# Scores of the second and third branch: one full f32 product a tile against three rounded products of high and low parts

## What is computed

```python
# second branch: 8 heads of 128, keys picked by an index (top 128 of 512, causal)
score = where(kpos <= t, sum_h iw_h * relu(iq_h . ik), -inf);  idx = top_k(score)
s = (q . k[idx]) * 128 ** -0.5 + bias;  p = masked_softmax(s);  o_b = p @ v[idx]

# third branch: 8 heads in 2 groups, three sources of keys: compressed (31 blocks),
# selected blocks (here all), window (here all causal keys)
o_c = softmax(q . k_cmp * scale, cmask) @ v_cmp
o_s = softmax(q . ks * scale + bias) @ vs
o_w = softmax(q . kw * scale + wbias) @ vw
o = gate0 * o_c + gate1 * o_s + gate2 * o_w
```

## Time and profile before

| | |
|---|---|
| median of 3 runs | 1434.14 us |
| the profiled execution | 1434.28 us, its span 1432.5 us |
| PE | busy 1421.0 us, 99% of the span, 7066 matmuls |
| DVE, ACT | busy 771.7 and 617.5 us, 54% and 43% |
| granted PE clock, mean | 0.999 |

### The profile page before, as it was taken

The page is one execution under the profiler, slowest core; times in us unless marked ns, Lnnn a source line. Parts: engine busy times, 40 slices in busy tenths (PEclk is TensorE's granted clock), DMA queues, the critical chain, the costliest instruction groups (busy, mean ns, idle before and its releaser), DMA issues.

```text
span 1432.5 us, 17397 instructions
## 1 busy us (share of the span) xinstructions
PE 1421.0 (99%) x7066; PEld 1156.6 (81%) x7066; DVE 771.7 (54%) x1326; ACT 617.5 (43%) x1013; POOL 82.8 (6%) x69
## 2 busy tenths in 40 slices
PE   9999999999999999999999999999999999999998
PEld 8867778887888888886777788887779888888886
DVE  6577857855243364465355244573355645656545
ACT  4455541225234343355346324453343654535342
POOL 0000000022120001000000110000000101001000
PEclk9999999999999999999999999999999999999999
DMA  6210223222322244541110424253123995768511
GB/s 202 64 46 32 74 89 117 89 88 75 102 65 82 70 145 150 176 132 45 31 59 30 162 88 147 90 176 103 59 89 127 244 239 139 197 172 184 168 74 59
DMA packets 127938, 160.42 MB, mean 112 GB/s; under 512 B 7365, under 2 KB 98754, under 8 KB 127603
## 3 DMA queue, kind: packets, MB, share of 16 engines
q1 hardware_dynamic: 117088, 133.51, 29.0%
q0 software_dynamic: 10624, 25.73, 8.3%
q10 hardware_dynamic: 146, 0.07, 0.0%
HBM read 155.06 MB, written 4.24 MB: 111 GB/s over the span
## 4 chain that ended last, share of the span: by engine, by line
PE 98%; DVE 1%; ACT 1%; issue 0%; DMA 0%; DVEq 0%; ACTq 0%
PE dense L809 24%; PE dense L811 24%; PE dense L810 24%; PE score L955 4%; PE score L972 3%; PE turned L972 3%; PE turned L955 2%; PE turned L965 1%; PE score L965 1%; PE score L809 1%; PE score L811 1%; PE score L810 1%; PE turned L811 1%; PE turned L809 1%; PE turned L810 1%; PE score L1126 1%
## 5 line engine op out<-in xcount | busy, mean ns | idle before, releaser
L809 PE MATMUL dense<-hidden_high,weight_high 128*128 128x512 f32 (+1 forms) x840 | 327.1, 389 | 0.0
L811 PE MATMUL dense<-hidden_high,weight_low 128*128 128x512 f32 (+1 forms) x840 | 320.7, 382 | 0.0
L810 PE MATMUL dense<-hidden_low,weight_high 128*128 128x512 f32 (+1 forms) x840 | 320.4, 381 | 0.0
L1495 ACT ACTIVATE weight_high<-raw 128x1024 fp32r<-128x1024 f32 (+5 forms) x178 | 211.9, 1227 | 218.5 <-PE dense L811 194.0
L2014 DVE TENSOR_TENSOR weight_low<-raw,weight_high 128x2048 fp32r<-128x2048 f32 (+2 forms) x78 | 158.9, 2046 | 192.5 <-ACT weight_high L1495 192.4
L811 PEld LDWEIGHTS dense<-hidden_high,weight_low 128*128 128x128 f32 x840 | 157.9, 188 | 30.8
L810 PEld LDWEIGHTS dense<-hidden_low,weight_high 128*128 128x128 f32 x840 | 158.2, 188 | 29.2 <-issue 0.5
L809 PEld LDWEIGHTS dense<-hidden_high,weight_high 128*128 128x128 f32 x840 | 158.1, 188 | 29.0 <-issue 0.5
L2009 DVE TENSOR_TENSOR weight_low<-raw,weight_high 128x1024 fp32r<-128x1024 f32 (+1 forms) x98 | 104.3, 1113 | 91.6 <-ACT weight_high L1495 91.6
L809 PE MATMUL dense<-weight_high,hidden_high 128*128 128x256 f32 (+1 forms) x288 | 82.0, 285 | 0.1
L811 PE MATMUL dense<-weight_high,hidden_low 128*128 128x256 f32 (+1 forms) x288 | 81.2, 282 | 0.0
(11 more groups left out here) (379 smaller groups left out, 2501.0 us busy)
## 6 DMA issues: line engine op xcount, KB each, us to landing
raw<-in_w_in SPq DMA_DIRECT2D x33, 1024.0 KB, 5.3
raw<-in_mlp_w SPq DMA_DIRECT2D x23, 1024.0 KB, 5.6
raw<-in_w_branch SPq DMA_DIRECT2D x12, 1024.0 KB, 5.3
down_raw<-in_mlp_w SPq DMA_DIRECT2D x12, 1024.0 KB, 6.1
raw<-in_mlp_w POOLq DMA_DIRECT2D x9, 1024.0 KB, 8.6
raw<-in_nsa_cmp_w SPq DMA_DIRECT2D x8, 1024.0 KB, 5.4
raw<-in_cross_wkv SPq DMA_DIRECT2D x8, 1024.0 KB, 5.2
down_raw<-in_mlp_w POOLq DMA_DIRECT2D x6, 1024.0 KB, 12.1
```

What stands on the lines that cost most here:

```text
L809: pe.matmul(out_ap, ah, bh, start=first, stop=False)
L810: pe.matmul(out_ap, ah, bl, start=False, stop=False)
L811: return pe.matmul(out_ap, al, bh, start=False, stop=last)
L1495: return nc.scalar.activation(dst, src, ACT.Copy, scale=scale)
```

## The change

Score tiles with 256, 384 and 512 keys, in the second and the third branch, are computed as three rounded products: high part of queries x high part of keys, high x low, low x high. Tiles with 128 keys, and the scores of the compressed keys, stay full f32 products, so the plain f32 values are kept as well: the first 128 tokens of queries and keys in the second branch, the first 128 of the keys and all of the queries (`qT`) in the third.

- ACT writes, per query product, a plain copy (256 elements a row in the second branch, 1024 as before in the third) and the rounded high part (1024).
- DVE waits for that (`query_high`), subtracts for the query's low part, and only this counts as the taking of the bank: the taker of `dq` and `nq` goes from "A" to "V".
- DVE writes three things per key product where it wrote one: the plain first 128 tokens, the high part, and, after waiting for it, the low part.
- In DVE's order, the query's low part stands ahead of the low part of slab + 2 and of the key's parts.
- The semaphore `up_relu_done`, which nothing used, gives its place to `query_high_ready`.

```diff
+        kTH = at("keys_high", [P, 2, T], 132, F32R)
+        dsaQ = [at("dsa_query_high", [P, 2, T], 128, F32R), at("dsa_query_low", [P, 2, T], 188, F32R), at("dsa_query_first", [P, 2, P], 196)]
+        dsaK = [kTH, at("dsa_key_low", [P, 2, T], 192, F32R), at("dsa_key_first", [P, 2, P], 197)]
+        nsaQ = [at("nsa_query_high", [P, 2, T], 178, F32R), at("nsa_query_low", [P, 2, T], 182, F32R), qT]
+        nsaK = [kTH, at("nsa_key_low", [P, 2, T], 200, F32R), at("nsa_key_first", [P, 2, P], 204)]
...
-            product(("dq", p), "A", slab_at["dq", p])
+            product(("dq", p), "V", slab_at["dq", p])
...
+            def split_terms(q, k, h, w, i):
+                rows, cols = slice(i * P, (i + 1) * P), slice(0, (i + 1) * P)
+                if i == 0:
+                    return [(q[2][:, h, rows], k[2][:, w, cols])]
+                return [(q[0][:, h, rows], k[0][:, w, cols]), (q[0][:, h, rows], k[1][:, w, cols]),
+                        (q[1][:, h, rows], k[0][:, w, cols])]
...
-                pe.wait_ge(taken["A"], taken_count[product_at["dq", p]])
+                pe.wait_ge(taken["V"], taken_count[product_at["dq", p]])
...
-                        score_tile((8 + 2 * p + h) * NT + j, [(qT[:, h, i * P:(i + 1) * P], kT[:, h, 0:(i + 1) * P])], (i + 1) * P)
+                        score_tile((8 + 2 * p + h) * NT + j, split_terms(dsaQ, dsaK, h, h, i), (i + 1) * P)
...
-                            score_tile(n, [(qT[:, h, i * P:(i + 1) * P], kT[:, w, 0:(i + 1) * P])], (i + 1) * P)
+                            score_tile(n, split_terms(nsaQ, nsaK, h, w, i), (i + 1) * P)
...
 # ScalarE, second branch
-                copy(qT[:, :, :], bank(("dq", p))[:, :, :], HEAD_SCALE).then_inc(taken["A"], 1)
+                copy(dsaQ[2][:, :, :], bank(("dq", p))[:, :, 0:P], HEAD_SCALE)
+                copy(dsaQ[0][:, :, :], bank(("dq", p))[:, :, :], HEAD_SCALE).then_inc(query_high, 1)
                 high(slab_at["dq", p] + 2)
...
 # ScalarE, third branch
             def nsa_query(p):
                 ready(("nq", p))
-                copy(qT[:, :, :], bank(("nq", p))[:, :, :], HEAD_SCALE).then_inc(taken["A"], 1)
+                copy(qT[:, :, :], bank(("nq", p))[:, :, :], HEAD_SCALE)
+                copy(nsaQ[0][:, :, :], bank(("nq", p))[:, :, :], HEAD_SCALE).then_inc(query_high, 1)
...
 # VectorE
+            def query_low(name, p, parts):
+                dve.wait_ge(query_high, p + 1 + (4 if name == "nq" else 0))
+                rest(parts[1][:, :, :], bank((name, p))[:, :, :], parts[0][:, :, :], HEAD_SCALE).then_inc(taken["V"], 1)
+
+            def key_parts(name, p, parts):
+                src = bank((name, p))
+                V.tensor_copy(parts[2][:, :, :], src[:, :, 0:P])
+                link(V.tensor_copy(parts[0][:, :, :], src[:, :, :]))
+                V.tensor_tensor(parts[1][:, :, :], src[:, :, :], parts[0][:, :, :].bitcast(F32), ALU.subtract).then_inc(taken["V"], 1)
+
             merge(0)
             for p in range(4):
+                query_low("dq", p, dsaQ)
                 low(slab_at["dq", p] + 2)
                 ready(("dk", p))
-                V.tensor_copy(kT[:, :, :], bank(("dk", p))[:, :, :]).then_inc(taken["V"], 1)
+                key_parts("dk", p, dsaK)
...
             def nsa_key(r):
                 ready(("kk", r))
                 dve.wait_ge(merge_added, GROUPS)
-                V.tensor_copy(kT[:, :, :], bank(("kk", r))[:, :, :]).then_inc(taken["V"], 1)
+                key_parts("kk", r, nsaK)
 
             for name, i in NSA_BEGIN:
+                if name == "nq":
+                    query_low("nq", i, nsaQ)
                 if name == "kk":
                     nsa_key(i)
                 if name != "vv":
                     low(slab_at[(name, *i) if name == "cw" else (name, i)] + 2)
...
             for p in range(4):
                 r = p // 2
+                if p:
+                    query_low("nq", p, nsaQ)
                 if p == 2:
                     low(slab_at["nq", p] + 2)
                     nsa_key(r)
```

More of the change, by code:

```diff
@@ L477, in layer @@
                 product("hidT", "A")
-            product((name, i), {"nq": "A", "kk": "V", "vv": "A"}[name], slab_at[name, i])
+            product((name, i), {"nq": "V", "kk": "V", "vv": "A"}[name], slab_at[name, i])
         product("cmp", "V")
         for name, i in (("nq", 1), ("nq", 2), ("kk", 1), ("vv", 1), ("nq", 3)):
-            product((name, i), {"nq": "A", "kk": "V", "vv": "A"}[name], slab_at[name, i])
+            product((name, i), {"nq": "V", "kk": "V", "vv": "A"}[name], slab_at[name, i])
         merge_products(2)
@@ L663, in layer @@
         up_ready = sem("up_ready")
-        up_relu_done = sem("up_relu_done")
+        query_high = sem("query_high_ready")
         up_summed = sem("up_sums_ready")
@@ L1207, in _ @@
                         nsa_v(r)
-                pe.wait_ge(taken["A"], taken_count[product_at["nq", p]])
+                pe.wait_ge(taken["V"], taken_count[product_at["nq", p]])
                 pe.wait_ge(taken["V"], taken_count[product_at["kk", r]])
```

## The result

The changed kernel takes 1436.57 us, the median of 20 runs (1435.59 to 1437.64); beside it the kernel before took 1434.43 (20 runs, 1433.99 to 1434.99). The ratio is 1.0015, interval 1.0008 to 1.0021: 0.15% slower. That is clear of the noise of 20 runs, and still inside the 0.2% that the prediction counts as no change. The profiled execution took 1436.6 us, its span 1434.8, 2.3 more than before.

A forecast was written before the change was run, and what follows sets the result against it. TensorE, busy 99% of the span, was taken as the bound. From 1434.28, less 6.2 in score bursts, plus 6.2 of waits and 1.9 for the clock, less 0.14 above the median: 1436.0 us; 8-in-10 range 1431.3 to 1439.0.

The forecast's parts named there:

- Matmul time: Score tiles, second and third branch: three rounded products for one full save 0.37 us in each of 24 sets, 8.8 us.
- What evictions take back: Score bursts: tiles wait for VectorE's eviction three tiles back, leaving 6.2 us saved, bounds 5.4 to 8.8.
- The walk: Tile-by-tile reckoning of score bursts, each tile no earlier than 0.32 us after the eviction three tiles back; gave 6.2 us saved.
- Hidden parts: Extra split work: zero in second branch and third-branch pair 2; pairs 1 and 3 together 0.1 us, each zero to 1.0.
- The gap ahead of key product 0: Third branch's opening: TensorE waits 4.5 us, the query's low part preceding the weights' on VectorE; bounds 3.5 to 5.5.
- The gap ahead of value product 0: Third branch's opening: three key instructions ahead of the weights' low part add 1.6 us of wait, bounds 1.2 to 2.0.
- The clock: TensorE's clock falls in the opening stall, key product 0 begins at half speed: 1.9 us, between zero and 4.8.
- Sum: Whole kernel: 1434.28 - 6.2 + 6.2 + 1.9 = 1436.2, less 0.14 above the median: 1436.0 us, 0.13% more.
- Matmul time alone: Rival, score bursts: no waits for evictions, clock kept, 8.8 us saved against 6.2 of stalls: 1431.5 us; chance 0.07.
- No stall at the opening: Rival, third branch: VectorE reaches the weights in time, only 1.6 + 0.1 us lost: 1429.6 us; chance 0.08.
- The clock low for all of 9.7 us: Rival, key product 0: 1.2 GHz throughout, 4.8 us lost, 1438.9 us; chance 0.26, shared with an unseen extra stall.
- Rounding without gain: Rival, score tiles: rounded products cost as much as full ones, bursts no shorter, about 1442 us; chance 0.01.

The follow-up runs named there:

- e3: Changed kernel with its split work kept, but each tile of 256 to 512 keys one full f32 product of the high parts: 1442.30 us, ratio 1.0056.
- e4: Changed kernel with two rounded products per tile of 256 to 512 keys, query low x key high left out: 1432.97 us, ratio 0.9990.
- e8: Kernel of e7 with tiles ordered 128, 384, 256, 512 keys, then 128, 512, 256, 384: 1425.73 us, ratio 0.9938.
- e7: Kernel of e5 with the low part of a head's output moved behind the last eviction of the scores: 1428.07 us, ratio 0.9955.
- e6: The change in the second branch alone, third branch as in the kernel before: 1432.43 us, ratio 0.9987.
- e1: Changed kernel with VectorE doing the weights' low part ahead of the query's at the third branch's opening: 1429.64 us, ratio 0.9968.
- e5: Kernel of e1, with third-branch key product 0 emptied by one plain copy and the keys' parts made after the weights' low part: 1428.59 us, ratio 0.9958.
- e2: Changed kernel with 18 unused rounded matmuls on TensorE ahead of key product 0 of the third branch: 1434.19 us, ratio 0.9999.
- e9: Kernel before the change (full f32 products) with e8's tile order and the head's low part behind the evictions: 1431.63 us, ratio 0.9981.

## Why the prediction was right

The mechanism came as described: a gain in the bursts and a loss at the opening of the third branch that are nearly equal, and a fall of the clock on top. Term by term:

- **Matmul time (8.8 us less at most).** The durations held: in the changed kernel's timeline products of 256, 384 and 512 columns start 0.12, 0.17 and 0.23 apart.
- **What evictions take back (6.2 left).** The bursts gave 2.09 + 4.20 = 6.29; e3 has 5.7 to 6.4 when only the rounded products are taken away. That evictions are the cause is shown by e4 (a third less matmul time for 3.6 us) and by e8, where only the order of tiles changes. Two sizes inside the term were off and cancel, which is luck: pair 0 of the second branch saved 0.52 and not 0.62, pairs 1 to 3 saved 0.53 each and not 0.46. The walk has 3.70 to 3.74 us for eight tiles without a low part between evictions; measured are 3.84 in pair 0, and 3.83 in the others with the low part (changed kernel) and without it (e7). So the walk left out 0.1 in every such burst, which no run here explains, and counted 0.15 or so for a low part that costs nothing there.
- **Hidden parts.** Second branch: e6 has 1.9 of the 2.1 us that its bursts are worth. From the first score of a pair to that of the next, less the burst, nothing moved (40.0 us before and after, pairs 1 to 2). In the third branch this distance grew by 0.02 us into pair 1 and 0.05 into pair 3, not 0.1 for both.
- **The gap ahead of key product 0 (4.5 us).** 4.4; the order on DVE is its cause, since e1 moves that alone. The low part took 1.23 us and not 1.28.
- **The gap ahead of value product 0 (1.6 us more).** 1.6, from 0.38 after the chunk's last matmul to 1.97; e5 closes it.
- **The clock (1.9 us, between 0 and 4.8).** It fell 2.5 us into the gap and was back 5.1 us after PE resumed: 2.5 us by distances, 2.4 by e2. The term was 0.6 too small, the largest miss of the sum. e1 and e2 show that the gap is what lets it fall. That it falls was argued from the end of the trace; the 1.9 was a choice between two bounds and not worked out, so it is partly luck that it came so near. Its upper bound took the slow transposes of the start for a low clock. The profile does not bear that out: in the kernel before it has the granted clock at 1.00 from 8 to 11 us. Why those transposes take twice their later time stays open.
- **Sum.** 1436.0 forecast, 1436.57 measured. In the profiled executions the change is +2.3 where the sum has +1.9: the clock is 0.6 more, and the other terms are off by 0.1 us or less each, mostly the other way.
- **Rivals.** Matmul time alone is out by e3 and e4. No stall at the opening: false, but e1 is that case made real, and its 1429.6 us was the number given for it. The clock low for all of 9.7 us did not come. Rounding without gain is out by the bursts.

## What to carry to other kernels

An extra split step must be put behind, not ahead of, the work that the busiest engine asks for next: here the same instructions cost 7 us in one order and nothing in the other, because two queues (ScalarE's and VectorE's) were chained in front of one wait. In this kernel a gap of 4.4 us on TensorE cost another 2.4 through its clock. And where an engine at 99% writes into a few rotating places, walk the tiles with their evictions before counting on matmul time: here they kept 2.5 of 8.8 us.

The order of the tiles is a gain of its own. An order without short tiles side by side gave 2.3 us in the kernel with rounded products (e8), and with full ones too: e9 is 2.7 under the kernel before, the moved low part included. So it does not bring back what evictions take from the rounding: with that order rounded products and their split work are worth 5.9 us (1431.63 to 1425.73), with the old one 5.7 (e5, 1434.31 to 1428.59) to 6.2 (e7).

## What the runs showed beside this

In e4's profiled run the clock fell a second time, although PE never stood for more than 0.23 us after its last gap. Ahead of the fall lie a burst with such short waits and 16 products of 31 columns; the stretches, with the clock in the same place as above:
```profile
665.20:674.80 9.60, 9.16 (x51) 6.68 (x50) 8.29 (x37) 9.42 (x27) 0.00 (x0) 1.00 0.01 2
675.00:678.20 3.20, 3.20 (x9) 2.47 (x8) 3.10 (x6) 1.89 (x9) 0.72 (x1) 0.50 0.38 116
678.50:683.00 4.50, 4.50 (x21) 3.70 (x20) 4.33 (x18) 0.00 (x0) 0.00 (x0) 1.00 0.76 244
```
That costs some 1.7 us there (an estimate: 3.4 us at half speed), and e4's eleven times spread over 3.1 us where e9's spread over 0.6. What made the clock fall there is open: no run changes those waits or those products alone. The changed kernel has the same 16 products behind a burst with fewer waits, and no fall there.

What the long gap costs through the clock differs too. The same 4.4 us gap stands in the profiled executions of e3 and e4, and the clock was low in each, but it fell 2.5 us after PE stopped in the changed kernel, 2.9 in e3 and 3.4 in e4, and was still low for 5.1, 5.5 and 5.9 us of the key product: 2.6 to 3.0 us lost, by half of that time. The changed kernel's 20 times spread over 2.0 us and those of before over 1.0, which fits a fall whose moment differs from run to run, but that was not shown on one kernel.
